# A transformer block with 16384 experts on one core: norm applied in the transposes, queries of four heads at once, residual kept on chip, six of the last sixteen V rows on VectorE

## The chip, the core and the metric

The kernel runs on one core of a Trainium2 chip. The metric is the device time of one execution in microseconds (us), median of several runs. TensorE multiplies, VectorE and ScalarE work on tiles of 128 partitions, GpSimd (POOL) here issues only DMAs whose row numbers are read from memory (gathers), SyncE (SP) issues plain DMAs. Each engine runs its own program in order; they meet at semaphores.

## The reference, cut to what matters

The block has a first half (modulation, attention, a recurrent branch, a short convolution, an output projection) that the change leaves alone but for its last stage. The second half is a layer of experts picked for each of 256 tokens:

```python
x = x + m_lat[2] * merge_branches(...)                 # the residual, "x2" below
hx = modulate(rmsnorm(x, norm_ffn), m_lat[3], m_lat[4])
x = x + m_lat[5] * peer_ffn(hx, peer_wq, peer_k1, peer_k2, peer_u, peer_v)

def peer_ffn, for 8 heads:
    q = hblk @ w_q                                     # two halves of 128 per head
    s1, s2 = q[..., 0, :] . k1, q[..., 1, :] . k2      # 128 keys each
    v1, i1 = top_k(s1, 16); v2, i2 = top_k(s2, 16)
    score, pos = top_k(v1 + v2 (16 x 16), 16)          # 16 experts of 16384
    gate = softmax(score)
    act = gelu(w_u[idx] . hblk)                        # a row of 2048 for each expert
    out += (gate * act) @ w_v[idx]                     # another row of 2048
```

For each head, token and k, one row of U and one of V (8 KB each) is read: 8 heads x 256 tokens x 16 x 2 rows, 537 MB in all.

## The kernel before, in words

The 256 tokens are two tiles of 128 (t = 0, 1). One gather brings row k of all 128 tokens of a tile: 128 x 2048 floats, 1.05 MB. There are 256 U gathers and 256 V gathers. U lands in a ring of 4 slots, V in a ring of 8. For each U gather VectorE forms the dot product with the token's normed row hN (line 1595); when the 16 of a tile are there it makes 16 weights wt (lines 1602 to 1611, with a sigmoid on ScalarE, line 1032). ScalarE makes a diagonal matrix dg from each weight (line 1039), and TensorE multiplies it with the V slot, four matmuls of 512 columns (line 736), summing in PSUM banks 0 to 3. After 16 rows VectorE adds the four banks to acc (line 1615), and the first row of the next tile waits for this add.

The last stage of the first half (WO) makes x2. TensorE uses weight pieces that ScalarE (line 781) and VectorE (line 1083) split into a high and a low part; four buffers of each lie between. Two column chunks of 512 are ready at once for both tiles: VectorE scales and adds them (lines 1504, 1506). Then, on one chain: x2 is stored to memory by ScalarE's queue (line 1005), ScalarE squares the two tiles with a sum (line 1009), a square root (line 1011), VectorE's reciprocal, hN in two halves by a multiply and an add for each tile (lines 1518, 1520), 32 transposes on TensorE (line 699) with 16 copies from PSUM on ScalarE (line 1015), the query projection of head 0 (line 711, 16 k-tiles x 2 blocks), its copy (line 1024), scores (line 722), top-k on VectorE (route, lines 1524 to 1587), and the first gather (line 1661). VectorE does the top-k of both tiles before its first dot product. The projection weights come in pieces of 1.05 MB, two per head, through four slots W by SP: head h + 2 is loaded when head h's projection has used its slots (line 377).

POOL's order is written out (lines 1655 to 1692): 16 U gathers of head 0, tile 0, with four V after the fourth; then turns, in which a U gather of one tile alternates with a V gather of the tile before. A U gather waits for the dot product that frees its slot, a V gather for the TensorE row that frees its slot; a waiting gather holds up all behind it. In the last head's second tile there are V gathers alone. At the end acc is multiplied by m5 and the residual is added, after it was read back from memory (lines 1051, 1626, 1628), and stored (line 395).

## Time and profile before

| | us |
|---|---|
| median of 3 runs | 3104.57 (3101.61 to 3104.84) |
| the profiled execution, time | 3104.09 |
| the profiled execution, span | 3102.3 |

| engine | busy us | share of the span |
|---|---|---|
| TensorE (PE) | 2675.0 | 86% |
| VectorE (DVE) | 1909.1 | 62% |
| ScalarE (ACT) | 912.5 | 29% |
| GpSimd (POOL) | 600.8 | 19% |

The span is that of the one execution whose trace is read below; its time has 1.8 us around it. Starts in the trace count from the start of the span. The first half ends at 1692.8 us, the first gather is issued at 1744.04. In a line of the timeline, the bracket at the end says how long the engine sat idle before the instruction and what released it.

### The profile page before, as it was taken

How to read it: one execution, taken by the hardware profiler on the slowest of the kernel's cores; microseconds unless marked ns; L12 is line 12 of the kernel's file. 1: busy time of each engine (PE TensorE's matmuls, PEld its weight loads, DVE VectorE, ACT ScalarE, POOL GpSimd, SP SyncE). 2: the span in 40 equal slices, each digit the busy share in tenths (PEclk: the TensorE clock that was granted, in tenths of full speed). 3: DMA queues.
4: the chain of work that ended last, by engine and by line, in shares of the span. 5: the costliest groups of instructions: out<-in, count | busy, mean ns of one | idle time of the engine just before them, and what ended most of it. 6: DMA issues, size and time to landing. Idle time of an engine off the chain costs nothing.

```text
span 3102.3 us, 32041 instructions
## 1 busy us (share of the span) xinstructions
PE 2675.0 (86%) x11089; PEld 1816.9 (59%) x11089; DVE 1909.1 (62%) x2600; ACT 912.5 (29%) x1241; POOL 600.8 (19%) x580
## 2 busy tenths in 40 slices
PE   8899997999989999999998466869697887887778
PEld 3488875878767789998876423333343343343323
DVE  2389997443665768887545566655555565566552
ACT  1167775432554333333433110101011111111100
POOL 0000000000000000000000255334353434443341
PEclk9999998999999999999999788989899899999999
DMA  8633333542424868887564699999999999999996
GB/s 331 226 126 108 122 112 132 190 165 95 143 88 160 345 265 344 344 315 285 204 240 182 249 410 407 421 412 422 421 408 421 401 422 408 422 399 421 422 421 282
DMA packets 126625, 906.83 MB, mean 292 GB/s; under 512 B 14016, under 2 KB 15552, under 8 KB 16704
## 3 DMA queue, kind: packets, MB, share of 16 engines
q0 software_dynamic: 82944, 604.02, 47.3%
q1 hardware_dynamic: 38304, 278.94, 24.2%
q10 hardware_dynamic: 5280, 22.72, 1.9%
q8 instruction: 44, 0.72, 0.1%
q14 instruction: 53, 0.43, 0.0%
HBM read 901.39 MB, written 4.23 MB: 292 GB/s over the span
## 4 chain that ended last, share of the span: by engine, by line
PE 45%; DMA 29%; DVE 12%; issue 9%; ACT 3%; POOL 1%; DVEq 0%; ACTq 0%; POOLq 0%
DMA u<-in_peer_u,idx 28%; PE ps L425 9%; PE ps L468 8%; PE ps L470 8%; PE ps L469 7%; PE ps L736 6%; PE ps L483 3%; DVE u L1595 2%; DVE wl L1083 2%; PE ps L440 1%; DVE ub L1167 1%; ACT wh L781 1%; PE ps L622 1%; POOL v L1668 1%; DVE tt L1178 1%
## 5 line engine op out<-in xcount | busy, mean ns | idle before, releaser
L736 PE MATMUL ps<-v,dg 128*128 128x512 f32 x2048 | 931.1, 611 | 195.2 <-DMA v<-in_peer_v,idx 98.6
L1595 DVE SCALAR_TENSOR_TENSOR u<-u,hN 128x2048 f32<-128x2048 f32 x256 | 586.3, 2292 | 483.8 <-DMA u<-in_peer_u,idx 472.5
L736 PEld LDWEIGHTS ps<-v,dg 128*128 128x128 f32 x2048 | 392.6, 196 | 729.4 <-issue 586.0
L1083 DVE TENSOR_TENSOR wl<-w,wh 128x1024 fp32r<-128x1024 f32 x432 | 524.8, 1222 | 414.6 <-ACT wh L781 413.8
L781 ACT ACTIVATE wh<-w 128x1024 fp32r<-128x1024 f32 x432 | 453.5, 1058 | 685.8 <-PE ps L470 418.7
L1661 POOL DMA_INDIRECT u<-in_peer_u,idx x256 | 283.7, 1108 | 878.8 <-DVE u L1595 458.0
L425 PE MATMUL ps<-both,wh 128*128 128x256 f32 x2048 | 372.2, 285 | 5.4 <-DVE y L1295 5.1
L1039 ACT ACTIVATE dg<-con,wt 128x128 f32<-128x128 f32 x256 | 99.0, 399 | 849.7 <-PE ps L736 844.6
L425 PEld LDWEIGHTS ps<-both,wh 128*128 128x128 f32 x2048 | 320.8, 193 | 10.2 <-issue 9.1
L1668 POOL DMA_INDIRECT v<-in_peer_v,idx x256 | 282.9, 1105 | 184.0 <-PE ps L736 99.9
L1653 POOL DMA_DIRECT2D mr<-in_wmod x64 | 34.0, 532 | 1401.4 <-DVE br_lo L1423 980.1
L425 PE MATMUL ps<-both,wl 128*128 128x256 f32 x1024 | 290.3, 283 | 0.0
L468 PE MATMUL ps<-wh,both 128*128 128x512 f32 x640 | 263.4, 411 | 13.8 <-DVE wl L1083 10.3
L470 PE MATMUL ps<-wh,both 128*128 128x512 f32 x640 | 251.4, 393 | 0.0
L469 PE MATMUL ps<-wl,both 128*128 128x512 f32 x640 | 251.0, 392 | 0.0
L425 PEld LDWEIGHTS ps<-both,wl 128*128 128x128 f32 x1024 | 197.2, 193 | 0.0
L440 PE MATMUL ps<-both,wh 128*128 128x512 f32 x512 | 161.8, 397 | 9.6 <-DVE both L1146 8.6
L468 PE MATMUL ps<-wh,br_hi 128*128 128x512 f32 x384 | 150.8, 393 | 4.1 <-DVE wl L1083 3.2
L469 PE MATMUL ps<-wl,br_hi 128*128 128x512 f32 x384 | 150.1, 391 | 0.0
L470 PE MATMUL ps<-wh,br_lo 128*128 128x512 f32 x384 | 150.0, 391 | 0.0
L468 PEld LDWEIGHTS ps<-wh,both 128*128 128x128 f32 x640 | 121.4, 190 | 45.9 <-DVE wl L1083 11.7
L1263 DVE SCALAR_TENSOR_TENSOR mr<-mr,srow 128x2048 f32<-128x2048 f32 x64 | 146.1, 2283 | 2.4 <-DMA mr<-in_wmod 2.4
(224 smaller groups left out, 2730.3 us busy)
## 6 DMA issues: line engine op xcount, KB each, us to landing
w<-in_stream SPq DMA_DIRECT2D x264, 1024.0 KB, 4.8
mr<-in_wmod POOLq DMA_DIRECT2D x64, 1024.0 KB, 6.8
wg<-in_gates ACTq DMA_DIRECT2D x8, 512.0 KB, 3.5
u<-in_peer_u,idx POOLq DMA_INDIRECT x256, 16.8
v<-in_peer_v,idx POOLq DMA_INDIRECT x256, 18.0
xs<-in_ctx ACTq DMA_DIRECT2D x1, 2048.0 KB, 17.1
xs<-in_x ACTq DMA_DIRECT2D x1, 2048.0 KB, 23.0
x<-in_x ACTq DMA_DIRECT2D x1, 2048.0 KB, 7.9
```

Source lines behind the costliest of these rows:

```text
L425: last = mm(ps[:, bank, c0:c0 + T], w[:, kk, cols], src[part_][:, k, :], start=(k == 0 and bank not in started), stop=(k == KT - 1), skip_ ...
L440: last = mm(ps[:, banks + blk, :].rearrange("p (s t) -> p s t", s=2), w[:, kk, cols], both[:, :, part_, k, :], start=(k == 0 and n == 0), ...
L468: mm(ps[:, bank + i, :], of[0][:, k, rows], hi[:, kk, :], start=(k == 0), stop=False)
L469: mm(ps[:, bank + i, :], of[0][:, k, rows], lo[:, kk, :], start=False, stop=False)
L470: last = mm(ps[:, bank + i, :], of[1][:, k, rows], hi[:, kk, :], start=False, stop=(k == KT - 1))
L736: last = mm(ps[:, b, :], dg[:, k % 4, :], V[n % NV][:, b * 512:(b + 1) * 512], start=(k == 0), stop=(k == TOPK - 1))
L781: fn(wh[p % SPLITS][:, :, :], W[s][:, q * PIECE:(q + 1) * PIECE, :], ACT.Copy).then_inc(hi_done, 1)
L1083: tt(wl[p % SPLITS][:, :, :], W[s][:, q * PIECE:(q + 1) * PIECE, :], wh[p % SPLITS][:, :, :].bitcast(F32), ALU.subtract)\
L1263: stt(mr[n % NM][:, :], mr[n % NM][:, :], 1.0, srow[:, :], ALU.mult, ALU.mult, accum_out=mcols[:, n:n + 1])\
L1595: stt(U[n % NU][:, :], U[n % NU][:, :], 1.0, hN[:, t, :], ALU.mult, ALU.mult, accum_out=dot[:, t, k:k + 1])\
L1661: nc.gpsimd.indirect_dma_start(out=U[n % NU][:, :], out_offset=None, in_=a_u, in_offset=bass.IndirectOffsetOnAxis(ap=idx[:, odd, t, k:k + ...
L1668: nc.gpsimd.indirect_dma_start(out=V[n % NV][:, :], out_offset=None, in_=a_v, in_offset=bass.IndirectOffsetOnAxis(ap=idx[:, odd, t, k:k + ...
```

## The change

- Norm: ScalarE squares x2 in the four column chunks, each as soon as it is final; VectorE adds the partial sums. hN is at first only x2 times the reciprocal root (tile 0 on ScalarE, tile 1 on VectorE), so that the transposes can start; the gain and the shift are applied while the transposed tiles are copied out of PSUM, with a scale and a bias per partition (gcol, mcb, from columns that VectorE made earlier), every second one on VectorE. The full hN for the dot products is made by VectorE behind the transposes. The clearing of acc and the making of the gain row gfr move up into the WO stage.
- Queries: heads 0 to 3 are projected one after another at the start, each into a PSUM bank of its own; later head h + 4 is projected in the turn of head h. The weights of heads 2 and 3 go to four new slots WX, in the place of the split buffers, as soon as the first half's last piece is used. Three query buffers instead of one.
- VectorE's first dot product comes after the top-k of tile 0; the top-k of tile 1 goes four steps ahead and then between the dot products. POOL issues 2 + 2 + 4 V gathers among head 0's first 16 U gathers, the third group behind a wait for head 3's projection, and the first turn begins with V row 8.
- Residual: x2 stays on chip, neither stored nor read back.
- Last 16 V rows (head 7, tile 1): k = 1, 3, 5, 7, 9, 11 are multiplied and added by VectorE into acc, the other ten on TensorE in banks 4 to 7, which need not wait for the add of banks 0 to 3; each bank is finished and stored by itself.
- TensorE's and ScalarE's programs for the heads are written out instead of looped.

```diff
+            sp.wait_ge(piece_used, 2 * WQ0)
+            for s in range(4):
+                sp.dma_start(WX[s][:, :, :], a_stream[WQ0 + 4 + s].rearrange("p (k n) -> p k n", n=CW)).then_inc(wx_in[s], 16)
+            for h in range(4, PH):
+                for s in (0, 1):
+                    sp.wait_ge(piece_used, 2 * (WQ0 + 2 * (h - 1 if h > 4 else 0) + s + 1))
+                    sp.dma_start(W[s][:, :, :], a_stream[WQ0 + 2 * h + s].rearrange("p (k n) -> p k n", n=CW)).then_inc(arrived[s], 16)
...
+            route(0)
             scores(0, True)
-            route(0, 2)
+            route(1)
+            route(2)
             scores(1)
-            with pe.Fori(0, PH // 2 - 1) as i:
-                for odd in (0, 1):
-                    experts(i * 2 + odd, 0)
-                    route(i + 1, 2 * odd)
-                    scores(i * 2 + (2 + odd))
-                    experts(i * 2 + odd, 1)
-            experts(PH - 2, 0, 1)
-            experts(PH - 1, 0, 1)
+            route(3)
+            pe.wait_ge(*AR.at(3, "q"))
+            for h in range(PH):
+                experts(h, 0)
+                if h + 4 < PH:
+                    route(h + 4)
+                if h + 2 < PH:
+                    scores(h + 2)
+                if h + 1 < PH:
+                    experts(h, 1)
+            last_half()
...
+            def last_half():
+
+                for j, k in enumerate(ON_PE):
+                    n = TOPK + k
+                    pe.wait_ge(v_in[n % NV], (PH - 1) * (2 * TOPK // NV * 16) + 16 * (n // NV + 1))
+                    pe.wait_ge(last_dg, j + 1)
+                    for b in range(4):
+                        last = mm(ps[:, 4 + b, :], dg[:, j % 4, :], V[n % NV][:, b * 512:(b + 1) * 512], start=(j == 0), stop=(k == TOPK - 1))
+                        if k == TOPK - 1:
+                            last.then_inc(last_bank, 1)
+                    if k < TOPK - 1:
+                        last.then_inc(last_pe, 1)
...
+            def squares(c):
+
+                for t in (0, 1):
+                    act.wait_ge(*VW.at(c // 2, f"a{c % 2}{t}"))
+                    if c:
+                        act.wait_ge(*AF.at(0, f"sq{c - 1}{t}"))
+                    fn(junk2[:, t, :], x2[:, t, c * WIDE:(c + 1) * WIDE], ACT.Square, accum_out=fsq[:, t, c:c + 1]).then_inc(*AF.inc(f"sq{c}{t}"))
...
+            squares(NW - 1)
+            act.wait_ge(*VF.at(0, "ss"))
             fn(fst[:, 2:4], fst[:, 0:2], ACT.Sqrt, scale=1.0 / D, bias=tiny[:, 1:2]).then_inc(*AF.inc("rt"))
-            act.dma_start(keys[:, :, :], a_keys[0].rearrange("p (s n) -> p s n", s=2)).then_inc(keys_in, 16)
-            for k in range(KT):
...
+            for k in range(1, KT, 2):
                 act.wait_ge(*PF.at(0, f"hT{k}"))
-                fn(hT[:, k, :], ps[:, 4 + k % 4, 0:T], ACT.Copy).then_inc(*AF.inc(f"hT{k}"))
-            act.wait_ge(*VF.at(0, "ha11"))
+                fn(hT[:, k, :], ps[:, 4 + k % 4, 0:T], ACT.Identity, scale=gcol[:, k:k + 1], bias=mcb[:, KT + k:KT + k + 1]).then_inc(*AF.inc(f"hT{k}"))
...
+            queries(0)
             gates(0, 0)
+            queries(1)
+            load_keys(1)
+            queries(2)
             gates(0, 1)
-            queries(1)
+            queries(3)
             gelus(0, 0)
-            with act.Fori(0, PH - 2) as h:
+            for h in range(PH):
                 turn(h)
-            turn(PH - 2, queries_too=False)
-            turn(PH - 1, more=False, queries_too=False)
+            act.wait_ge(*VE.at(PH - 1, "w1"))
+            for j, k in enumerate(ON_PE):
+                act.wait_ge(*(last_used(ON_PE[j - 4]) if j >= 4 else PE_.at(PH - 1, f"v0{TOPK - 4 + j}")))
+                fn(dg[:, j % 4, :], ident, ACT.Copy, scale=wt[:, 1, k:k + 1]).then_inc(last_dg, 1)
...
+                    nc.vector.memset(acc[:, :, :], 0.0).then_inc(*VF.inc("acc0"))
+                    dve.wait_ge(rows_in, 48)
+                    stt(gfr[:, :], m4r[:, :], 1.0, gfr[:, :], ALU.add, ALU.mult).then_inc(*VF.inc("g1"))
+
+            dve.wait_ge(*AF.at(0, f"sq{NW - 1}1"))
+            nc.vector.reduce_sum(fst[:, 0:2], fsq[:, :, :], AX.X).then_inc(*VF.inc("ss"))
             dve.wait_ge(*AF.at(0, "rt"))
-            nc.vector.reciprocal(fst[:, 4:6], fst[:, 2:4]).then_inc(*VF.inc("rc0"))
-            dve.wait_ge(*VF.at(0, "rc0"))
+            nc.vector.reciprocal(fst[:, 4:6], fst[:, 2:4]).then_inc(*VF.inc("rc"))
+            dve.wait_ge(*VF.at(0, "rc"))
             for half in (0, 1):
                 cols_ = slice(half * D // 2, (half + 1) * D // 2)
-                for t in (0, 1):
-                    stt(hN[:, t, cols_], x2[:, t, cols_], fst[:, 4 + t:5 + t], gfr[:, cols_], ALU.mult, ALU.mult).then_inc(*VF.inc(f"hm{t}{half}"))
-                    dve.wait_ge(*VF.at(0, f"hm{t}{half}"))
-                    tt(hN[:, t, cols_], hN[:, t, cols_], m3r[:, cols_], ALU.add).then_inc(*VF.inc(f"ha{t}{half}"))
-            nc.vector.memset(acc[:, :, :], 0.0).then_inc(*VF.inc("acc0"))
-            dve.wait_ge(*VF.at(0, "acc0"))
+                tsc(hN[:, 1, cols_], x2[:, 1, cols_], fst[:, 5:6], None, ALU.mult).then_inc(*VF.inc(f"x1{half}"))
+            for k in range(0, KT, 2):
+                dve.wait_ge(*PF.at(0, f"hT{k}"))
+                tsc(hT[:, k, :], ps[:, 4 + k % 4, 0:T], gcol[:, k:k + 1], mcb[:, KT + k:KT + k + 1], ALU.mult, ALU.add).then_inc(*VF.inc(f"hT{k}"))
+            dve.wait_ge(*PF.at(0, f"hT{KT - 1}"))
+            for t in (0, 1):
+                tt(hN[:, t, :], hN[:, t, :], gfr[:, :], ALU.mult).then_inc(*VF.inc(f"hm{t}"))
+                dve.wait_ge(*VF.at(0, f"hm{t}"))
+                tt(hN[:, t, :], hN[:, t, :], m3r[:, :], ALU.add).then_inc(*VF.inc(f"ha{t}"))
...
+            def last_row(k):
+
+                j, n = ON_DVE.index(k), TOPK + k
+                dve.wait_ge(v_in[n % NV], (PH - 1) * (2 * TOPK // NV * 16) + 16 * (n // NV + 1))
+                if j:
+                    dve.wait_ge(last_dve, j)
+                stt(acc[:, 1, :], V[n % NV][:, :], wt[:, 1, k:k + 1], acc[:, 1, :], ALU.mult, ALU.add).then_inc(last_dve, 1)
...
+            for _ in range(4):
+                next(second)
+            dots(0, 0, second)
             dots(0, 1, route(1, 0, 1, False))
...
+            last_row(1)
             add(PH - 1, 0)
-            final(0)
-            add(PH - 1, 1)
-            final(1)
+            dve.wait_ge(last_in, 16)
+            dve.wait_ge(*VA.at(PH - 1, "ac0"))
+            tt(acc[:, 0, :], acc[:, 0, :], m5r[:, :], ALU.mult).then_inc(*VX.inc("m"))
+            last_row(3)
+            dve.wait_ge(*VX.at(0, "m"))
+            tt(acc[:, 0, :], acc[:, 0, :], x2[:, 0, :], ALU.add).then_inc(*VX.inc("o"))
+            for k in ON_DVE[2:]:
+                last_row(k)
+            dve.wait_ge(last_dve, len(ON_DVE))
+            tt(acc[:, 1, :], acc[:, 1, :], m5r[:, :], ALU.mult).then_inc(*VX.inc("m1"))
+            dve.wait_ge(*VX.at(0, "m1"))
+            tt(acc[:, 1, :], acc[:, 1, :], x2[:, 1, :], ALU.add).then_inc(*VX.inc("p1"))
+            for b in range(4):
+                cols_ = slice(b * WIDE, (b + 1) * WIDE)
+                dve.wait_ge(last_bank, b + 1)
+                tt(U[0][:, cols_], ps[:, 4 + b, :], m5r[:, cols_], ALU.mult).then_inc(*VX.inc(f"x{b}"))
+                dve.wait_ge(*VX.at(0, f"x{b}"))
+                tt(acc[:, 1, cols_], acc[:, 1, cols_], U[0][:, cols_], ALU.add).then_inc(*VX.inc(f"o{b}"))
...
+                if last and n >= TOPK + NV:
+                    pool.wait_ge(*last_used(k - NV))
...
+                    rows_v(0, 0, 0, 0)
+                    rows_v(0, 0, 0, 1)
+                if k == NU + 2:
+                    pool.wait_ge(piece_used, 2 * (WQ0 + 4))
+                    rows_v(0, 0, 0, 2)
+                    rows_v(0, 0, 0, 3)
+                if k == NU + 8:
+                    pool.wait_ge(piece_used, 2 * (WQ0 + 8))
+                    for kv in range(4, 8):
                         rows_v(0, 0, 0, kv)
-            turn(0, 0, begun=4)
+            turn(0, 0, begun=8)
```

## Rows read from the trace of the kernel before

**Rows 1.** Busy time by stretch: five engines, TensorE clock share, DMA share, GB/s

```profile
1744.00:3030.00 1286.00, 970.96 (x2364) 453.63 (x2363) 762.58 (x1188) 142.73 (x321) 555.09 (x503) 0.91 1.00 414
```

**Rows 2.** Chain that ended last, gather stage: one longer link, one typical

```profile
2052.48 22.11 DMA u<-in_peer_u,idx
...
2138.68 16.75 DMA u<-in_peer_u,idx
```

**Rows 3.** Timeline of the end: POOL, VectorE, TensorE

```profile
3012.87 2.48 POOL L1668 DMA_INDIRECT v<-in_peer_v,idx  x1 [0.30 <-issue]
3027.16 2.29 DVE L1595 SCALAR_TENSOR_TENSOR u<-u,hN 128x2048 f32<-128x2048 f32 x1 [2.67 <-DMA u<-in_peer_u,idx]
3029.66 3.70 PE L736 MATMUL ps<-v,dg 128*128 128x512 f32 x8 [1.27 <-DMA v<-in_peer_v,idx]
3035.83 55.17 PE L736 MATMUL ps<-v,dg 128*128 128x512 f32 x128 [2.47 <-DVE acc L1615]
3091.04 2.29 DVE L1615 TENSOR_TENSOR acc<-acc,ps 128x2048 f32<-128x2048 f32 x1 [40.78 <-PE ps L736]
3095.68 2.29 DVE L1628 TENSOR_TENSOR acc<-acc,x2b 128x2048 f32<-128x2048 f32 x1
```

**Rows 4.** Timeline of VectorE and ScalarE after WO: x2, squares, root, hN, clearing

```profile
1694.97 0.69 DVE L1506 TENSOR_TENSOR x<-x,xm 128x512 f32<-128x512 f32 x1
1698.60 1.91 ACT L1009 ACTIVATE junk<-x 128x2048 f32<-128x2048 f32 x1
1701.91 0.29 ACT L1011 ACTIVATE fst<-fst,tiny 128x2 f32<-128x2 f32 x1
1702.44 1.28 DVE L1518 SCALAR_TENSOR_TENSOR hN<-x,fst,gfr 128x1024 f32<-128x1024 f32 x1
1713.15 3.47 DVE L1521 MEMSET acc<- 128x4096 f32 x1 [0.80 <-issue]
```

**Rows 5.** Timeline of TensorE: transposes, then head 0's queries

```profile
1707.49 3.67 PE L699 MATMUL ps<-con,hN 128*128 128x128 f32 x16 [14.73 <-DVE hN L1520]
1712.40 3.68 PE L699 MATMUL ps<-con,hN 128*128 128x128 f32 x16 [1.24 <-DVE hN L1520]
1716.55 14.08 PE L711 MATMUL ps<-hT,w 128*128 128x256 f32 x64 [0.47 <-ACT hT L1015]
```

**Rows 6.** Busy time by stretch, as in group 1: the transposes, then behind them

```profile
1707.00:1716.00 9.00, 7.27 (x32) 6.55 (x32) 8.13 (x6) 5.69 (x15) 0.00 (x0) 0.50 0.00 0
1716.00:1724.00 8.00, 7.53 (x36) 6.57 (x36) 0.62 (x1) 0.46 (x2) 0.00 (x0) 0.97 0.39 131
```

**Rows 7.** Timeline of POOL: the first gather, V row 8; landing of U by source line

```profile
1744.04 0.99 POOL L1661 DMA_INDIRECT u<-in_peer_u,idx  x1 [308.19 <-DVE tv L1531]
1817.09 2.19 POOL L1668 DMA_INDIRECT v<-in_peer_v,idx  x1 [0.30 <-PE ps L736]
...
DMA to landing us min/median/max: 5.6/8.7/15.8
```

**Rows 8.** Timeline of VectorE, end of WO: the two splits behind the second chunk

```profile
1655.87 1.23 DVE L1083 TENSOR_TENSOR wl<-w,wh 128x1024 fp32r<-128x1024 f32 x1 [0.30 <-ACT wh L781]
1658.59 1.23 DVE L1083 TENSOR_TENSOR wl<-w,wh 128x1024 fp32r<-128x1024 f32 x1 [1.49 <-ACT wh L781]
```

**Rows 9.** Page, costliest groups: ScalarE's splits

```profile
L781 ACT ACTIVATE wh<-w 128x1024 fp32r<-128x1024 f32 x432 | 453.5, 1058 | 685.8 <-PE ps L470 418.7
```

**Rows 10.** Timeline: last dot of the first tile, TensorE, ScalarE, the fifth dot after

```profile
1803.21 2.29 DVE L1595 SCALAR_TENSOR_TENSOR u<-u,hN 128x2048 f32<-128x2048 f32 x1 [0.39 <-DMA u<-in_peer_u,idx]
1807.50 50.78 PE L736 MATMUL ps<-v,dg 128*128 128x512 f32 x112 [46.97 <-ACT dg L1039]
1813.51 0.40 ACT L1039 ACTIVATE dg<-con,wt 128x128 f32<-128x128 f32 x1 [5.28 <-PE ps L736]
1826.11 2.29 DVE L1595 SCALAR_TENSOR_TENSOR u<-u,hN 128x2048 f32<-128x2048 f32 x1 [1.68 <-DMA u<-in_peer_u,idx]
```

**Rows 11.** Source line of SP's weight loads from 1700 us on: first and last

```profile
L377 SPq DMA_DIRECT2D w<-in_stream x12: 333/333/334, 1723.9 to 2395.0; - x12
```

More of the change, by code:

```diff
@@ L115, in build @@
         m_flat = m_dram.rearrange("r (c n) -> (r c) n", n=P)
-        x2_dram = nc.dram_tensor("x2_rows", [2, P, D], F32, kind="Internal").ap()
         def sem(name):
@@ L356, in build, with last_used @@
         PE_ = Steps(sem("pe_experts"), [f"v{t}{k}" for t in (0, 1) for k in range(TOPK)], primed=True)
-        VX = Steps(sem("dve_last"), ["m0", "o0", "m1", "o1"])
+        VX = Steps(sem("dve_last"), ["m", "o", "m1", "p1"] + [f"{w}{b}" for b in range(4) for w in "xo"])
+        ON_DVE = (1, 3, 5, 7, 9, 11)
+        ON_PE = tuple(k for k in range(TOPK) if k not in ON_DVE)
+        last_pe, last_dve, last_bank, last_dg = sem("last_pe"), sem("last_dve"), sem("last_bank"), sem("last_dg")
+        def last_used(k):
+            return (last_dve, ON_DVE.index(k) + 1) if k in ON_DVE else (last_pe, ON_PE.index(k) + 1)
         PRIMED_V = [VM, VT, VL] + VO + [VS, VW, VE, VA]
@@ L700, in _, with route @@
                 last.then_inc(*PF.inc(f"hT{k}"))
-            pe.wait_ge(*AF.at(0, f"hT{KT - 1}"))
-            def route(turn, slot0):
+            def route(h):
                 for q in (0, 1):
-                    s = slot0 + q
-                    pe.wait_ge(arrived[s], turn * 16 + 16 * (WQ0 // RING + 1))
+                    if h < 2:
+                        w, in_, n = W[2 * h + q], arrived[2 * h + q], 16 * (WQ0 // RING + 1)
+                    elif h < 4:
+                        w, in_, n = WX[2 * h + q - 4], wx_in[2 * h + q - 4], 16
+                    else:
+                        w, in_, n = W[q], arrived[q], 16 * (WQ0 // RING + h - 2)
+                    pe.wait_ge(in_, n)
+                    if h > 4 and q == 0:
+                        pe.wait_ge(*AR.at(h - 1, "q"))
                     for kk in range(HK):
                         k = q * HK + kk
+                        if h == 0:
+                            pe.wait_ge(*evicted(k))
                         for blk in (0, 1):
-                            last = mm(ps[:, 4, blk * T:(blk + 1) * T], W[s][:, kk, blk * P:(blk + 1) * P], hT[:, k, :],
+                            last = mm(ps[:, min(h, 4), blk * T:(blk + 1) * T], w[:, kk, blk * P:(blk + 1) * P], hT[:, k, :],
                                       start=(k == 0 and blk == 0), stop=(k == KT - 1), skip_group_check=True)
@@ L1000, in _ @@
                 split(WO0, 0, 16, p)
+                if p == 14:
+                    squares(0)
             for p in range(5, 16):
                 split(WO0, 1, 16, p)
[L1003 to L1009 removed]
@@ new lines, in _, with load_keys @@
+            act.wait_ge(*VF.at(0, "rc"))
+            for half in (0, 1):
+                cols_ = slice(half * D // 2, (half + 1) * D // 2)
+                fn(hN[:, 0, cols_], x2[:, 0, cols_], ACT.Copy, scale=fst[:, 4:5]).then_inc(*AF.inc(f"x0{half}"))
+            def load_keys(h):
+                if h:
+                    act.wait_ge(*PR.at(h - 1, "s1"))
+                act.dma_start(keys[:, :, :], a_keys[h].rearrange("p (s n) -> p s n", s=2)).then_inc(keys_in, 16)
+            load_keys(0)
@@ L1678, in turn @@
                         rows_u(h + 1, 1 - odd, 0, k)
-                    rows_v(h, odd, 1, k)
-            pool.wait_ge(*VF.at(0, "ha11"))
+                    rows_v(h, odd, 1, k, not more)
             for k in range(TOPK):
```

114 lines of the change are left out of this document (53 added, 61 removed).

## The prediction

> **What bounds the kernel now.** I read the busy time by stretch first. From the first gather to the last dot product (1744 to 3030) the DMA engines are busy all the time, 414 GB/s on average, and TensorE has air [rows 1]. The chain of waits says the same: U gathers of mostly 16.75 us between short steps [rows 2]. A gather is 1.05 MB; dot products at the end of the stage start every 4.97 us (2.29 busy, 2.67 idle) and cover one U and one V gather [rows 3], so one transfer takes 2.5 us. Three parts have to be costed: what lies ahead of the first gather, what the DMA engines carry or miss until the last dot, and the tail behind it, where 128 matmuls run without a pause [rows 3] and only TensorE counts.
>
> **A, the way to the first gather: 10 us less.** Before: x2 is complete at 1695.66; squares, table load and root run to 1702.20; four multiply and add pairs lie between 1702.44 and the second half of the transposes at 1712.40; head 0's queries start at 1716.55 [rows 4, 5]. After: the last chunk's square of 512 columns costs a quarter of 1.91 us and some 0.3 around it, to 1696.5. The root comes 1.4 us behind the last square as before (1700.51 to 1701.91, a table load in it; the small sum of VectorE hides behind that load), and ends at 1698.2. Reciprocal 0.25; scaling the first half on two engines at once at most 1.28 (the old multiply did more). Transposes start at 1699.7 and not 1707.49: 7.8 us less. They lose the pause of 1.24 us and the last copy's 0.47 [rows 5]: 1.7 less. Copies go to two engines, so TensorE stays the slower. The clock is granted at 0.50, so 1.2 GHz, during both halves and 0.97 behind them [rows 6]; it rose when the second 16 transposes had run without a pause. Here all 32 do, so I take 2.4 GHz by the queries at the latest, with some of the transposes quicker (up to 2 us). Sum 7.8 + 1.7 + 0.5 = 10. From the queries' end (1730.63) to the first gather lie 13.4 us of scores and top-k [rows 5, 7]; this is as before. Bounds: nothing lost from the clock and 2 us won, -12; the queries entirely at 1.2 GHz cost 14 us more, +4.
>
> The full hN, four operations of 2.3 us on VectorE, begins behind the transposes at about 1707 and ends at 1716; VectorE is next wanted when the queries and scores are through, at 1722. Cost nothing, cover 6 us.
>
> The clearing of acc (3.47 us [rows 4]) and gfr (2.3 like every VectorE operation of 2048 columns) go into WO, ahead of the split of piece 21 [rows 8]. Without them that split starts at 1655.87, with them 5.8 later at 1661.6, and it ends at 1662.8. TensorE needs the piece five pieces of 2.72 us after the chunk's end at about 1649.2 (the second split's 1658.59 is the same distance behind the first, 2.72), so at 1662.8. It just fits; later splits win back 1.49 us each [rows 8]. I take 0; if the cover is short, up to 2 us. ScalarE's squares, 1.6 us a chunk, fit beside splits of 1.06 in 2.72 [rows 9]. The removed stores of x2 were on no one's path but POOL's V gathers, which came later.
>
> **B, the start of the gathers: 8.5 us more.** G is the first gather's start. A first landing takes 5.6 us [rows 7]. TensorE's queries of heads 1 to 3 and two scores (3 x 14.1 + 2 x 1.2 = 44.7 us from 13.4 before G) end at G + 31.3. POOL waits for them behind U12, which waits for dot 8; U8 is the 13th transfer, lands at G + 35.6 and its dot ends at G + 38. So this wait costs nothing. But POOL's first turn now starts with U'0 (tile 1), then V8, and V8 waits for the first TensorE row of head 0. Transfers ahead: 16 U, 8 V, U'0. With 2.5 us each U15 lands at G + 63, its dot ends at T = G + 65.5, and U'0 has landed by then too. From the last dot's end (1805.43) TensorE starts 2.1 us later, and its first row frees the slot 6.0 us after that, at 1813.51 [rows 10]. V8 is then issued at T + 8.3 = G + 73.8 and lands at G + 79.4. U'1 is queued behind V8 on POOL, so VectorE has nothing either. The DMA engines stand idle from G + 65.6 to 76.9, 11 us.
>
> Before, V8 was issued at G + 73.1 in a full queue and the dot on U'4 began at G + 82.1 [rows 7, 10]; V8, one transfer ahead, landed at G + 79.6. So at the same distance from G, the kernel before has 20 U and 9 V, the new one 17 U and 9 V. It lacks three gathers, 7.5 us; with 1 us for the slower filling between top-k steps 8.5. Bounds: 0 (if the queue is somehow never dry) and 11 + 1.
>
> **C, weights: 5.4 us less.** SP issues twelve pieces from 1723.9 to 2395.0 [rows 11]: heads 2 to 7. Those of heads 4 to 7 come during the gathers; each pair makes one link of the chain 22.11 instead of 16.75 us, so 5.4 a pair [rows 2]. In the new kernel heads 2 and 3 are loaded from 1692.8 and head 4 behind head 0's queries, with idle DMA engines; heads 5 to 7 remain. One pair less. (The piece of head 3 that fell just behind the first gather is in the count of B, which compares with what really landed.)
>
> **D, the tail: 20.3 us less.** L is the last dot's end, 3029.4 before (3027.16 + 2.29). The kernel before ends at L + 72.9. Now V0 of the last tile (issued 3012.87) is next in the queue behind V15 of tile 0, used at L + 0.3 [rows 3], so V0 lands at L + 2.7 and Vk 2.5k later, V15 at L + 40.2, if its slot is free. Slots: TensorE ends tile 0 at L + 4.0, then row 0 at 7.5 (3.45 us a row, 55.17 / 16), 2 at 11.2, 4 at 16.2, 6 at 21.2; VectorE does row 1 to 7.5, the add and the first multiply to 12.1, row 3 to 14.4, the second add, rows 5 to 19.0 and 7 to 22.5. V15's slot is free at 22.5, 17.7 us before V15 would land; the queue stays full. The removed read-back of x2 (2.1 MB) no longer stands in that queue. TensorE then follows the landings: rows 8, 10 end at 26.2, 31.2, row 12 at 36.1, and 13, 14, 15 back to back at 39.6, 43.0, 46.4. VectorE is through with row 11 and two whole-row operations at 37.1. Bank 0 is ready at 44.0; four banks of two operations of 0.69 us and a little around them, 5.8, give L + 50. The last store is 4.3 us for 1.05 MB before (3097.97 to the span's end); a quarter of the bytes saves 1.9: L + 52.6. So 72.9 - 52.6 = 20.3. Bounds: 17 to 23.
>
> A gather's issue took 0.99 us with VectorE in short steps, 2.19 beside dot products [rows 7]; the tail now has VectorE at work there. Eight late issues cost at most 10 us, under the 17.7 in hand. The Trainium skill, page SBUF — State Buffer, section "SBUF: two separate sides", says that a VectorE operation with two SBUF inputs and a GpSimd operation that reads SBUF exclude each other for their whole length. By that rule VectorE's own rows would wait as well and the tail could lose some us; the issue row agrees in kind.
>
> **The sum.** -10 + 8.5 - 5.4 - 20.3 = -27.2 from the profiled execution's 3104.09 (span 3102.3 and 1.8): 3076.9, said as 3077. The execution is 0.5 under the median of the runs, so the two can be compared.
>
> **Rivals.** (1) The queue doesn't run dry at the start: PE's first row or POOL's order turns out harmless. Against: the wait stands in program order. 3077 - 8.5 = 3068.5. (2) The clock stays low into the queries. For: 0.50 right up to 1716 [rows 6]. Half of the queries at 1.2 GHz is 7 us: 3084. (3) The tail pays: VectorE and POOL exclude each other, ten operations each 0.9 us later, then the banks begin late: 3084; should the six rows save nothing beyond TensorE's freed wait (the change doesn't do what it says), 13 us of TensorE rows come back: 3090. (4) Slower: POOL's dry queue returns at each of the fifteen later tile turns, because V gathers wait for TensorE and U gathers lie behind them. It needs 27.2 / 15 = 1.8 us of idle DMA at each to undo everything; at 3 us each the time is 3122. Against: the turns' order is unchanged from head 1 on, and the share was 1.00 there [rows 1]. TensorE's longer program, written out, could do the same by fetching; no row shows it.
>
> **Chances.** Forecast 0.68, (1) 0.10, (2) 0.08, (3) 0.08 with 0.03 of it at 3090, (4) 0.04; a mix of (2) and (3) near 3100 has 0.02. Range 3065 to 3087: it holds the forecast with its bounds (about 7 us either way), (1), (2) and the milder part of (3). 0.2% of the time, 6 us, is about what a measurement of this kernel can tell from no change: faster 0.94, within 0.02, slower 0.04.
>
> **What would show it.** Right: transposes starting about 1700 and the first gather at 1734; DMA share near 0 for some 11 us around G + 70 and a wait of POOL for TensorE there; three links of 22 us instead of four; the last dot near 3022.6; TensorE's last row 46 us behind it. Wrong: a first gather later than 1738 (A), no dry stretch (B), a DMA share under 0.98 in later turns (rival 4), TensorE rows in the tail waiting for dg or a landing longer than 1.6 us each (D), or TensorE waiting for a split near 1662 in WO.

## The result, and the profile after

| | before | after |
|---|---|---|
| median of the runs, us | 3103.2 (4 runs, 3101.61 to 3104.84) | 3082.11 (4 runs, 3080.03 to 3083.83) |
| ratio, 95% interval | | 0.993 [0.9915, 0.9946] |
| the profiled execution, time and span, us | 3104.09, 3102.3 | 3083.66, 3081.8 |
| busy: TensorE, VectorE, us | 2675.0, 1909.1 | 2660.0, 1930.2 |
| busy: ScalarE, GpSimd, us | 912.5, 600.8 | 912.0, 599.6 |

The change saves 21 us, where 27 had been forecast; 3082.1 lies inside the range of 3065 to 3087. Four points cut both spans into the parts of the prediction: the end of x2, the first gather G, the end of the last dot product L, and the end of the span.

| us | before | after | difference | forecast |
|---|---|---|---|---|
| end of x2 | 1695.66 | 1692.73 | -2.9 | 0 |
| end of x2 to G | 48.38 | 36.31 | -12.1 | -10 (A) |
| G to L | 1285.41 | 1298.07 | +12.7 | +8.5 - 5.4 = +3.1 (B, C) |
| L to the end | 72.85 | 54.69 | -18.2 | -20.3 (D) |

So the total is off by 6 us and would be off by more: a miss of 10 us in the middle is half covered by the first two rows, and the 2.9 us of the first are chance, as the repeated traces below show. Each row has to be looked at for itself.

**The way to the first gather.** The timeline of the kernel after, ScalarE and TensorE, where [rows 4, 5] answer for before; then the busy time by stretch as in [rows 6] (stretch, its length, busy time of PE, PEld, DVE, ACT, POOL, granted clock, DMA share, GB/s):

```profile
1692.76 0.63 ACT L1051 ACTIVATE junk<-x 128x512 f32<-128x512 f32 x1 [0.73 <-DVE x L1575]
1694.80 0.29 ACT L1063 ACTIVATE fst<-fst,tiny 128x2 f32<-128x2 f32 x1
...
1696.53 5.55 PE L720 MATMUL ps<-con,hN 128*128 128x128 f32 x32 [6.71 <-ACT hN L1067]
1701.91 13.98 PE L740 MATMUL ps<-hT,w 128*128 128x256 f32 x64
```

```profile
1696.50:1699.00 2.50, 2.47 (x12) 2.47 (x13) 1.37 (x4) 2.04 (x3) 0.00 (x0) 0.50 1.00 423
1699.00:1702.00 3.00, 3.00 (x23) 2.44 (x22) 2.63 (x6) 2.71 (x6) 0.00 (x0) 0.93 0.95 391
```

The transposes start 3.80 us behind the end of x2 (11.83 before), and 32 of them with the change to the queries take 5.38 us (9.06 before). The clock stood at 0.50, that is 1.2 GHz, for the first of them and at 0.93 on average from 1699 on, mostly 2.4 GHz, after TensorE had worked without a pause from 1696.53. When it rises differs between executions of the same instructions: in nine traces of kernels with these transposes (all but the one with the squares behind x2, below) they took 5.3 to 5.4 us in seven and 6.2 to 6.3 us in two.

**The start of the gathers.** The timeline of the kernel after: POOL's first two gathers of the first turn, U'0 (the prime marks tile 1) and V8, then dot 15 and the dots of U'0 and U'1 on VectorE, and TensorE's first rows:

```profile
1786.22 0.94 POOL L1755 DMA_INDIRECT u<-in_peer_u,idx  x1 [0.31 <-issue]
1807.80 0.94 POOL L1765 DMA_INDIRECT v<-in_peer_v,idx  x1 [20.65 <-PE ps L765]
...
1797.14 2.29 DVE L1670 SCALAR_TENSOR_TENSOR u<-u,hN 128x2048 f32<-128x2048 f32 x1 [0.19 <-DMA u<-in_peer_u,idx]
1800.66 2.28 DVE L1670 SCALAR_TENSOR_TENSOR u<-u,hN 128x2048 f32<-128x2048 f32 x1
1816.67 2.29 DVE L1670 SCALAR_TENSOR_TENSOR u<-u,hN 128x2048 f32<-128x2048 f32 x1 [13.72 <-DMA u<-in_peer_u,idx]
...
1801.43 43.33 PE L765 MATMUL ps<-v,dg 128*128 128x512 f32 x96 [41.35 <-ACT dg L1100]
```

This is the cycle that was forecast: V8 waits 20.65 us for TensorE's first row, U'1 stands behind V8, and VectorE waits 13.72 us for U'1. What it costs is read from the busy time by stretch, cut at equal distances from the first gather: G to G + 68, to 82.1, to 120, to 172, then the rest of the stage. First after:

```profile
1729.04:1797.04 68.00, 31.03 (x148) 27.09 (x146) 42.87 (x68) 3.48 (x6) 34.42 (x25) 0.76 0.96 383
1797.04:1811.14 14.10, 9.71 (x19) 4.33 (x20) 5.39 (x9) 2.30 (x7) 1.88 (x2) 0.71 0.18 60
1811.14:1849.04 37.90, 33.62 (x79) 14.61 (x77) 19.01 (x35) 3.69 (x7) 19.52 (x16) 1.00 1.01 414
1849.04:1901.04 52.00, 29.74 (x96) 18.95 (x96) 37.14 (x56) 4.82 (x13) 27.80 (x19) 0.80 0.94 375
...
1900.00:3026.00 1126.00, 871.66 (x2024) 389.94 (x2024) 656.98 (x1021) 128.83 (x288) 468.13 (x440) 0.92 1.00 414
```

and the same four stretches of the kernel before:

```profile
1744.04:1812.04 68.00, 8.84 (x25) 5.37 (x24) 49.58 (x78) 3.77 (x9) 43.32 (x27) 0.55 0.96 383
1812.04:1826.14 14.10, 14.10 (x34) 6.25 (x33) 8.32 (x20) 1.60 (x4) 11.66 (x9) 1.00 1.01 426
1826.14:1864.04 37.90, 35.83 (x83) 15.22 (x81) 24.55 (x41) 5.96 (x12) 13.07 (x13) 1.00 1.01 422
1864.04:1916.04 52.00, 22.69 (x86) 16.95 (x87) 31.69 (x47) 1.97 (x6) 23.64 (x18) 0.74 1.00 411
```

Up to G + 68 both move 383 GB/s. Then the new kernel moves 60 against 426 GB/s for 14.1 us: 5.16 MB less, at the stage's 414 GB/s 12.5 us. The third stretch adds 0.3 MB, 0.7 us; the fourth, where the share is 0.94 and not 1.00, 36 x 52 = 1.9 MB, 4.5 us. Together 7.3 MB, 17.7 us. From 1900 on the share is 1.00, as in [rows 1].

Not all of these bytes are gathers. SyncE's timeline of the kernel before has a weight piece of 1.05 MB (head 3's second) behind its first gather at 1744.04; in the kernel after, all pieces up to head 4's are issued before the first gather:

```profile
1746.47 0.33 SPq L377 DMA_DIRECT2D w<-in_stream  x1
```

So of the 17.7 us, 2.5 are this piece, which the new kernel need not load here, and 15.2 are missing gathers: 4 of them up to G + 82.1 (29.6 against 25.6).

**The weights.** The chain of waits, its links over 19 us in the gather stage of the kernel after (columns start, length, what), then the first such link of the kernel before:

```profile
1888.94 20.07 DMA u<-in_peer_u,idx
...
2053.73 22.12 DMA u<-in_peer_u,idx
...
2221.99 22.09 DMA u<-in_peer_u,idx
```

```profile
1889.21 18.46 DMA u<-in_peer_u,idx
```

Each starts between 0.3 us before and 14 us after SyncE issues a pair of pieces (1875.36, 2053.83 and 2222.11 after; 1875.31, 2052.79, 2219.51 and 2388.07 before). Before there were this link of 18.46 and three like the first of [rows 2], for four pairs; after there are three: one pair less.

**The tail.** The timeline of the kernel after, TensorE, VectorE, POOL's issue of V8 and SyncE, where [rows 3] answer for before; L is 3027.11:

```profile
3030.86 3.60 PE L776 MATMUL ps<-v,dg 128*128 128x512 f32 x8
3051.86 24.19 PE L776 MATMUL ps<-v,dg 128*128 128x512 f32 x48 [3.43 <-DMA v<-in_peer_v,idx]
...
3047.20 2.35 DVE L1703 SCALAR_TENSOR_TENSOR acc<-v,wt,acc 128x2048 f32<-128x2048 f32 x1 [1.16 <-DMA v<-in_peer_v,idx]
3054.56 2.35 DVE L1703 SCALAR_TENSOR_TENSOR acc<-v,wt,acc 128x2048 f32<-128x2048 f32 x1 [5.01 <-DMA v<-in_peer_v,idx]
3073.51 0.69 DVE L1736 TENSOR_TENSOR u<-ps,m5r 128x512 f32<-128x512 f32 x1 [6.97 <-PE ps L776]
3078.22 0.69 DVE L1738 TENSOR_TENSOR acc<-acc,u 128x512 f32<-128x512 f32 x1
...
3035.27 0.95 POOL L1765 DMA_INDIRECT v<-in_peer_v,idx  x1 [2.50 <-DVE acc L1703]
...
3043.81 0.34 SPq L412 DMA_DIRECT2D out<-acc  x1
```

```profile
3051.00:3055.00 4.00, 3.14 (x4) 1.51 (x5) 0.44 (x1) 0.00 (x0) 0.60 (x1) 0.51 1.01 426
```

V8 of the last tile is used at L + 24.75 and not 22.7. TensorE idles 3.43 us before it, VectorE then 5.01, and in the next 4 us the granted clock is 0.51. SyncE had issued the store of out[0], 1.05 MB, at 3043.81: 8.5 us behind the issue of V8, but 8 us ahead of V8's use. (POOL's line names VectorE's row 1 as what released V8; its slot is that of row 0 on TensorE, which ended 0.3 us before.) TensorE's last row ends at L + 48.9, VectorE's last add at L + 51.8.

### The profile page after: what moved, and what is told of

The parts are those of the page before. It is cut to its first block, busy times and chain, and to the rows that moved or that the text cites. A ratio compares the mean times of both kernels' runs of the same rounds, so it can differ in the third digit from the quotient of the medians.

```text
span 3081.8 us, 31629 instructions
## 1 busy us (share of the span) xinstructions
PE 2660.0 (86%) x11041; PEld 1807.1 (59%) x11041; DVE 1930.2 (63%) x2622; ACT 912.0 (30%) x1241; POOL 599.6 (19%) x580
## 4 chain that ended last, share of the span: by engine, by line
PE 44%; DMA 29%; DVE 12%; issue 9%; ACT 3%; POOL 1%; DVEq 0%; ACTq 0%; POOLq 0%
DMA u<-in_peer_u,idx 27%; PE ps L445 9%; PE ps L488 7%; PE ps L490 7%; PE ps L489 7%; PE ps L765 5%; PE ps L503 3%; DVE u L1670 2%; DMA v<-in_peer_v,idx 2%; DVE wl L1148 2%; POOL v L1765 1%; PE ps L460 1%; ACT wh L827 1%; DVE ub L1232 1%; PE ps L642 1%
## 5 line engine op out<-in xcount | busy, mean ns | idle before, releaser
L765 PE MATMUL ps<-v,dg 128*128 128x512 f32 x1920 | 882.2, 616 | 188.5 <-DMA v<-in_peer_v,idx 92.7
L765 PEld LDWEIGHTS ps<-v,dg 128*128 128x128 f32 x1920 | 370.7, 197 | 695.9 <-issue 538.0
L1755 POOL DMA_INDIRECT u<-in_peer_u,idx x256 | 270.1, 1055 | 856.0 <-DVE u L1670 447.5
L1765 POOL DMA_INDIRECT v<-in_peer_v,idx x256 | 295.3, 1154 | 198.0 <-PE ps L765 111.5
```

Of the source, the lines that this page charges most:

```text
L765: last = mm(ps[:, b, :], dg[:, k % 4, :], V[n % NV][:, b * 512:(b + 1) * 512], start=(k == 0), stop=(k == TOPK - 1))
L1755: nc.gpsimd.indirect_dma_start(out=U[n % NU][:, :], out_offset=None, in_=a_u, in_offset=bass.IndirectOffsetOnAxis(ap=idx[:, odd, t, k:k + ...
L1765: nc.gpsimd.indirect_dma_start(out=V[n % NV][:, :], out_offset=None, in_=a_v, in_offset=bass.IndirectOffsetOnAxis(ap=idx[:, odd, t, k:k + ...
```

## The experiments

The theory after these traces: the time is gained on three paths, each counting one to one (A, C, D), and half of it is given back because V8, second in the first turn, starves the DMA engines. The rivals: the first turn is slow for another reason (POOL's issues beside VectorE, the DMA engines themselves); the shorter way to G is hidden; the rows on VectorE do nothing. Medians stand beside those of the kernel before in the same series: 3105.74 us (7 runs) for the first four kernels, 3103.41 (7 runs) for the next three, 3102.82 (7 runs) for the last two. The kernel after has two series of its own, 3082.11 beside 3103.2 and 3079.43 beside 3102.82, so a difference of 2 to 3 us between medians of different series says nothing; G to L and the tail, read from the traces, are steadier. The edits are against the kernel after.

**No block of V gathers ahead of the turn.** V8 is no longer the first V gather of the turn, V4 is, and its slot has never been used:

```
-                if k == NU + 8:
-                    pool.wait_ge(piece_used, 2 * (WQ0 + 8))
-                    for kv in range(4, 8):
-                        rows_v(0, 0, 0, kv)
-            turn(0, 0, begun=8)
+            pool.wait_ge(piece_used, 2 * (WQ0 + 8))
+            turn(0, 0, begun=4)
```

> The changed kernel with one thing put back: POOL issues only V rows 0 to 3 among head 0's first 16 U gathers, and the first turn begins with U'0, V4, U'1, V5 and so on, so that V8 is the fifth V gather of that turn and four U gathers of tile 1 go ahead of it. Theory (the dry queue): the loss at the start comes from V8 standing in front of U'1 while it waits for TensorE's first row. Then the DMA share has no dry stretch at the end of head 0's first tile, POOL's wait of 20.65 us there shrinks to under 5 us, and the time is that of the changed kernel less 11 to 18 us: 3064 to 3071. Rival (the filling): the loss comes from the top-k of tile 1 between the first dot products, which slows the U ring whatever POOL's order is; then the dry stretch only moves and the time is within 4 us of 3082.

Measured: 3064.96 us (3062.66 to 3067.43), ratio 0.9868 [0.9851, 0.9884]; 17 us less than the kernel after, 20 if each is compared with the kernel before in its own series. Busy time by stretch, G = 1733.03:

```profile
1801.03:1815.13 14.10, 14.10 (x34) 6.27 (x33) 8.17 (x13) 1.60 (x4) 11.66 (x9) 1.00 1.01 425
1815.13:1853.03 37.90, 34.63 (x80) 14.76 (x79) 22.64 (x42) 5.56 (x11) 12.18 (x13) 1.00 1.01 422
1853.03:1905.03 52.00, 22.78 (x86) 16.72 (x85) 31.96 (x46) 2.21 (x7) 22.78 (x17) 0.70 1.00 411
```

The dry stretch is gone, and so is the dip at G + 120 to 172. These are the numbers of the kernel before to within 1 GB/s. G to L is 1277.83, 20.2 less than after. Over all traces it is 1292.9 to 1298.1 (mean 1294.9) in the five kernels with this block and POOL's order unchanged, and 1276.5 to 1277.8 (mean 1277.4) in the three without it: the block costs 17.5 us. Against the kernel before it is 7.6 less, which is three weight pieces at 2.5 us: C's pair, and head 3's piece that fell behind G. So without the block nothing is lost at the start.

**U gathers first, the block kept.** Four U' gathers go ahead of V8, in the order in which their slots come free; all eight early V gathers stay:

```
-                for k in range(TOPK):
-                    rows_u(h, odd, 1, k)
-                    if k + begun < TOPK:
-                        rows_v(h, odd, 0, k + begun)
+                if begun:
+                    for k in range(NU):
+                        rows_u(h, odd, 1, k)
+                    for k in range(NU, TOPK):
+                        if k - NU + begun < TOPK:
+                            rows_v(h, odd, 0, k - NU + begun)
+                        rows_u(h, odd, 1, k)
...
```

> The changed kernel, but in the first turn the four U gathers of tile 1 whose slots are free go ahead of V8; the eight early V gathers stay. Theory (the dry queue): three more transfers lie in the queue while TensorE makes its first row, so 3 x 2.5 = 7.5 us of the 11 us dry stretch are filled and some 3 us of it stay: 3073 to 3076. If the pause of 12.0 us before dot 13, behind the block of four V gathers, is a cost of its own, four_early is another 3 to 8 us faster than this one; if it is not, the two differ by the 3 us only. Rival (the filling): within 4 us of 3082.

Measured: 3070.88 us (3069.62 to 3072.06), ratio 0.9888 [0.9871, 0.9904], 2 us under the expected range. POOL's timeline at the turn, then the stretch from G + 68 to 82.1 (G = 1731.48):

```profile
1796.41 2.49 POOL L1755 DMA_INDIRECT u<-in_peer_u,idx  x1 [7.37 <-DVE u L1670]
1809.59 2.45 POOL L1765 DMA_INDIRECT v<-in_peer_v,idx  x1 [6.96 <-PE ps L765]
```

```profile
1799.48:1813.58 14.10, 10.98 (x20) 4.85 (x21) 11.76 (x22) 2.30 (x7) 6.54 (x4) 0.71 0.70 241
```

POOL stands 6.96 us for TensorE instead of 20.65. The stretch still lacks (425 - 241) x 14.1 = 2.6 MB, 6.3 us, and the time is 5.9 us above the kernel without the block. So the order is two thirds of the loss. The rest stays as long as eight V gathers come early, which is the cost of its own that the expectation put at 3 to 8 us: the tile's last dot ends at G + 69.1 here and at G + 58.9 with four early V gathers, and TensorE's first row starts at G + 71.1 and not at 60.9.

**The store of out[0] later.** It waits for tile 1's second whole-row operation on VectorE, the last one before the banks, and so is no longer in flight beside the last V gathers:

```
-            sp.wait_ge(*VX.at(0, "o"))
+            sp.wait_ge(*VX.at(0, "p1"))
             sp.dma_start(out[0], acc[:, 0, :]).then_inc(stored, 16)
```

> The changed kernel, but the store of tile 0's output (1.05 MB) waits until tile 1's rows on VectorE are in and its first two whole-row operations are done, so that it no longer lies among the last V gathers. Theory: that store takes 2.5 us of the DMA engines just ahead of V row 8 of the last tile, which lands 2 us late; TensorE stands still for 3.4 us, its clock falls to 0.51 and row 8 runs at half speed. Without the store V8 lands 2.5 us earlier, the clock stays at 1.00, and from the last dot product to the end of the span it takes 52 us and not 54.7: a gain of 2 to 4 us, 3078 to 3080 in time. Rival: the landing is late because POOL's issues wait for VectorE (1.9 us each instead of 0.9); then V8's landing, the pause and the 54.7 us stay as they are.

Measured: 3077.67 us (3077.62 to 3078.62), ratio 0.9912 [0.9896, 0.9929]. TensorE's timeline and the busy time of the end; L is 3023.61:

```profile
3056.08 14.00 PE L776 MATMUL ps<-v,dg 128*128 128x512 f32 x32 [1.26 <-DMA v<-in_peer_v,idx]
```

```profile
3049.00:3055.00 6.00, 4.57 (x11) 1.48 (x9) 3.41 (x2) 0.55 (x2) 0.00 (x0) 1.00 1.03 425
```

Row 8 now starts at L + 22.6 (24.75 with the early store), though POOL issues V8 at the same L + 8.2 in both, and its issues beside VectorE still take 1.9 us: so it was the store, not POOL. The last row ends at L + 46.5, the forecast's 46.4; the clock stays at 1.00, and the tail is 52.19 us, 2.5 less. It is 52.2 in the three traces with the later store and 54.6 to 54.7 in the six with the early one and six rows on VectorE. The median fell by 4.4, the rest of it ahead of L, where nothing was edited.

**All sixteen last rows on TensorE.** The banks, the early store and the residual on chip stay:

```
-        ON_DVE = (1, 3, 5, 7, 9, 11)
+        ON_DVE = ()
...
-            last_row(1)
...
-            last_row(3)
```

> The changed kernel with all sixteen last V rows on TensorE, in banks 4 to 7 and without VectorE's six rows; the output by banks and the on-chip residual stay. Theory: TensorE's 16 rows of 3.45 us then run from 4 us behind the last dot without a pause, to L + 59, and the span ends at L + 65 to 66: 11 us more than the changed kernel, 3092 to 3094, and 7 us less than the kernel before, which is the share of the banks, of the store and of the residual. Rival: the V landings are the bound in the tail (the last one at about L + 42), so that sixteen rows on TensorE cost 3 to 5 us only: 3085 to 3087.

Measured: 3089.84 us (3087.91 to 3092.3), ratio 0.9953 [0.9936, 0.997]; tail 64.56 us. TensorE's timeline, L = 3021.54:

```profile
3025.28 55.10 PE L776 MATMUL ps<-v,dg 128*128 128x512 f32 x128
```

The median is 2 us under the expected 3092 to 3094 and the tail 0.4 under the expected 65: against the two series of the kernel after it is 7.7 and 10.4 us longer. The sixteen rows run without a pause and set the end. The six rows on VectorE are worth 64.56 - 54.69 = 9.9 us, and 12.4 with the later store. What is left of D, 72.85 - 64.56 = 8.3 us, can be read from the traces: the rows start at L + 3.7 and not at 6.4, without the wait for the add of banks 0 to 3 (2.6 us), and from their end to the span's end it takes 5.7 us and not 11.3 (5.6 us). How much of the 5.6 belongs to the finishing by banks, to the split store and to the residual kept on chip was not taken apart.

**Both fixes at once.** The first and the third edit:

> The changed kernel with both edits at once: only four V gathers ahead of the first turn, and the store of out[0] behind the issue of the last V gathers. The dry queue cost 17.2 us and the store 2.5 (tail 54.7 against 52.2 in the kernel with the later store alone); they lie in different stages, so the two should add: 3065.0 - 2.5 = 3062.5 us, a DMA share of 0.90 to 1.0 through the first tile turn and a tail of 52.2 us with TensorE at a granted clock of 1.0. A rival: the earlier last dot finds the store's place taken by something else, and the sum of the two is smaller: 3065.

Measured: 3063.14 us (3062.94 to 3065.51), ratio to the kernel before 0.9871 [0.9855, 0.9888]; the tail is 52.23 us. It beats the kernel before by 40 us and the changed one by 19. That it beats the kernel without the block by the whole 2.5 us isn't shown by the times (1.8 apart, with overlapping runs), only by the tails, 52.23 against 54.64.

**All squares at the end of ScalarE's program.**

```
-                if p == 14:
-                    squares(0)
...
-                if p in (6, 14):
-                    squares(p // 8 + 1)
-            squares(NW - 1)
+            for c in range(NW):
+                squares(c)
```

> The changed kernel, but ScalarE takes all its squares of x2 behind the last chunk instead of three of four between the splits. Theory, that the way to the first gather counts one to one: eight squares of about 0.63 us with some 0.2 around each stand between x2 and the root instead of two, so the transposes start 4.9 us later behind the end of x2 (8.7 instead of 3.8), the first gather 4.9 later behind it, the rest of the span as before, 3087. A rival: the first gathers are waited for by something else, or the splits gain what ScalarE no longer does beside them, and the time stays at 3082.

Measured: 3081.03 us (3080.78 to 3081.84), ratio 0.993 [0.9913, 0.9946]: no loss. The expected 3087 was wrong. ScalarE's timeline:

```profile
1683.47 0.62 ACT L1051 ACTIVATE junk<-x 128x512 f32<-128x512 f32 x1
1691.71 0.63 ACT L1051 ACTIVATE junk<-x 128x512 f32<-128x512 f32 x1 [7.53 <-DVE x L1572]
```

Six squares ran up to 1684, in the 11 us in which ScalarE, with all its splits done, waits for the last chunk. Where three of the four chunks are squared doesn't matter; that the last chunk alone is left does. The test added nothing to the path and says nothing of it.

**All squares behind the end of x2.** The same with a wait ahead, in the kernel with both fixes:

```
+            act.wait_ge(*VW.at(1, "a11"))
             for c in range(NW):
                 squares(c)
```

> Both fixes as in the kernel both_fixes, and all eight squares of x2 held back until x2 is complete. In squares_last the first six still ran before that, in ScalarE's idle 11 us ahead of the last chunk, and the time stayed. Here eight squares of 0.615 us each start at the end of x2, 4.99 us with 0.07 ahead of them; the last square ended 0.76 behind the end of x2 so far, so everything behind it begins 4.2 us later. Theory, one to one on the path: first gather 40.5 us behind the end of x2 instead of 36.3, and the time 3063.1 + 4.2 = 3067.3. A rival, that some of the way to the first gather is hidden: between 3063 and 3065.

Measured: 3067.01 us (3066.39 to 3072.1), ratio 0.9883 [0.9867, 0.99]; 3.9 us over the kernel with both fixes. The busy time during the transposes and behind them:

```profile
1707.00:1710.00 3.00, 2.78 (x13) 2.79 (x14) 1.87 (x4) 2.33 (x4) 0.00 (x0) 0.50 0.38 150
1710.00:1713.20 3.20, 3.20 (x22) 2.91 (x21) 2.44 (x6) 2.51 (x5) 0.00 (x0) 0.76 0.00 0
```

The first gather is issued 41.1 us behind the end of x2 and not 36.3: 4.3 from the squares, 0.5 because the clock rose later within the transposes, which it also does by 0.9 us between executions of unchanged code and so can't be put down to the edit. From G to L the two kernels differ by 1.2 us (1277.76 and 1276.54). So, within the 1 us by which such traces differ, the way to the first gather lies on the path one to one, and a saved microsecond there is a microsecond of the time.

**Without the query weights of heads 5 to 7.** Their queries use the weights of head 4, so six pieces of 1.05 MB aren't loaded and these heads pick other experts, by as many gathers of the same size:

```
-            for h in range(4, PH):
+            for h in range(4, 5):
...
-                        w, in_, n = W[q], arrived[q], 16 * (WQ0 // RING + h - 2)
+                        w, in_, n = W[q], arrived[q], 16 * (WQ0 // RING + 2)
```

> The changed kernel without the loads of the query weights of heads 5, 6 and 7; their queries are made with the weights of head 4, which are in the slots. So those heads pick other experts, but as many gathers of the same size run. Left out are six transfers of 1.05 MB. Theory: while the DMA engines are busy throughout, each pair costs 5.4 us, its link in the chain of waits being 22.1 instead of 16.7: three links of 22 us become 16.7, and the time is 3082 - 16.2 = 3066. A rival: the loads slip into idle DMA time and TensorE or VectorE set the pace, then it stays within 5 us of 3082.

Measured: 3064.73 us (3064.62 to 3067.84), ratio 0.9877 [0.986, 0.9893]: 17.4 us less than the first series of the kernel after and 14.7 less than the second, 16.2 expected. The chain of waits where the two long links of 22 us were:

```profile
2049.14 17.12 DMA u<-in_peer_u,idx
...
2211.62 17.18 DMA u<-in_peer_u,idx
```

The third link, 20.07 at 1888.94, is 15.05. The three links are shorter by 5.0 us each, and G to L is 1280.06, 14.8 under the mean of the five traces with the same order of the gathers. So a pair, two transfers of 2.5 us in a DMA queue that is never empty, costs 5.0 us, a little under the 5.4 that I took.

**The changed kernel once more.**

> The changed kernel once more, unaltered. The end of x2 lay 2.9 us earlier in its first trace than in the trace of the kernel before, and the stretch from the first gather to the last dot product was 1298.1 us, but 1295.3 and 1295.0 in two kernels that do the same up to there. Theory: neither is the change's work. The time stays at 3082 within 2 us, the end of x2 lies anywhere from 1692 to 1699, and the stretch is 1293 to 1298 us. A rival: both numbers come again within 0.3 us, and then they belong to the code.

Measured: 3079.43 us (3076.75 to 3081.79), ratio 0.9926 [0.991, 0.9943]. Both the time and the end of x2 missed their expectation: 2.7 us under 3082 and not within 2, and 1689.87, outside 1692 to 1699. Over the ten profiled executions of changed kernels the end of x2 lay between 1689.87 and 1699.14, though they share the code up to there but for the place of the squares; and G to L was 1293.17. Neither the 2.9 us at the end of x2 nor the last 5 us of G to L belong to the change. Where the first half's spread comes from stays open; no experiment was made on it.

## Why the prediction was right or wrong, point by point

**What bounds the kernel: right.** From 1900 to the last dot the DMA share is 1.00 at 414 GB/s in both kernels, and six transfers less save about 15 us, six times 2.5.

**A: right, 2 us short.** -12.1 against -10, a tenth beyond the better of the bounds, -12 (in two other traces, with the clock rising later, -11.2). The start of the transposes came 8.0 us nearer to x2 (forecast 7.8). Transposes to queries gave 3.7 and not 2.2: the clock rose within the transposes, which was the bound and not the value I took. From the queries to G it was 27.1 us after 27.5. Rival (2), the clock low into the queries, didn't happen. The edits in WO: the split of a later piece starts late once, by 0.65 us (ScalarE's wait for TensorE is 2.31 where 1.66 is the rule, at 1662.72), inside the 0 to 2 that I gave. The trace's other 2.9 us, the earlier end of x2, are spread.

**B: the mechanism right, the size wrong by a factor of two.** The sum asks for G to L without C: 12.7 + 5.4 = 18.1 us (14.8 over the five traces with the same order), forecast 8.5, upper bound 12. V8 did wait for TensorE, U'1 behind it, so rival (1) is out, and the DMA engines idled 0.82 x 14.1 = 11.6 us where I had said 11. The step that failed is the next one, "It lacks three gathers, 7.5 us", in two ways that work against each other. First, the count of the kernel before has an order wrong: POOL issues U'4 at 1815.84 and V8 behind it at 1817.09, so V8 landed behind G + 82.1 and not at 79.6, and the count there is 20 U and 8 V. Second, the forecast let the new kernel go into the pause with too long a lead: 25 gathers by G + 65.6, where the kernel before, by its bytes, has 23. U15, the 24th transfer, landed at G + 68 and not at 63, for the mean rate up to there was 383 GB/s and not 414; T came at G + 70.4 and not 65.5, and the lead was one gather. A pause worth 4.9 gathers less a lead of one is 4 gathers, 10 us, up to G + 82.1, where three and 7.5 us stood in my sum. What the sum lacked altogether is the dip at G + 120 to 172, 4.5 us. With 0.7 us between the two it makes 15.2 us, near the 14.8 of the five traces; the other 3 of the 18.1 us lie further back, where the traces of one and the same order differ by up to 5. The pause itself, 11 us plus a restart, stood in my text as a bound and would have been the better price. Rival (4), the pause at every later turn, didn't happen: the share is 1.00 from 1900 on, also with TensorE's longer program.

**C: right, 0.4 us too much.** One pair less. The experiment without three pairs gives 14.7 to 17.4 us by the medians and 14.9 by the three links, for 16.2: 5.0 us a pair and not 5.4. Not every pair has a link of 22 us, as I wrote: head 4's had 18.46.

**D: right, 2 us too much.** -18.2 against -20.3, within 17 to 23. TensorE ended tile 0 at L + 3.9 (forecast 4.0), V8 came at 24.75 (22.7), the last row ended at 48.9 (46.4). The step that failed: "The queue stays full" was true, but I had only V gathers in it. The store of out[0], 1.05 MB, uses the same DMA engines, and V8, issued 8.5 us before it, still landed 2.2 us late; it was costed nowhere. The kernel before has this store beside its last V gathers too (issued at 3050.29), but there TensorE's rows ran back to back and waited for no landing. The pause then took the clock down, 0.51 and 0.63 in the next two stretches of 4 us, but that cost only some 0.3 us more: the last row ends 2.5 us later than with the late store. With the store later it came at 46.5. Rival (3) didn't happen: VectorE's rows took 2.35 us each beside POOL's issues of up to 1.96 us, and the rows saved 9.9 us. The Trainium skill, page SBUF — State Buffer, section "SBUF: two separate sides", has whichever of the two starts first hold the port for its whole instruction. In the trace POOL's issues in the tail double from 0.94 to 1.9 us beside VectorE, which agrees. That VectorE would wait as well doesn't show: its operations follow each other from 3034.64 to 3046.04 while POOL issues five gathers, and its 2.35 is near the 2.29 of a dot product. The loss falls on the engine with slack.

**The sum.** By the spans -20.5 against -27.2: A and the spread at the end of x2 gave 5.0 more, B took 9.6 more (of which some 3 are spread), D gave 2.1 less. That the total is not further off is in part luck: the 2.9 us at the end of x2 are no one's work. By the medians of both series of the kernel after, -21.1 and -23.4.

## What to carry to other kernels

An engine that issues gathers in program order must not meet a slot's wait before it has issued those gathers whose slots are free: filling a ring to its last slot early turns the next gather into a wait for the consumer, and puts everything behind it. Price a pause of the bounding engine by its idle time unless the lead with which it is entered is known, and check it by bytes moved at equal distances, taking out those that only one of the kernels has to move. Where work is moved or added, cost its transfers in the queue of the engine that bounds, stores too: here a store of 1 MB beside the last loads cost as much as a load.

## What the runs showed of the hardware

- 50 us behind the pause of 11.6 us of the DMA engines, 36 GB/s were missing over 52 us (375 against 411). The order of the issues gives a reason: with eight V gathers early, the first turn's last eight U gathers have no V gather between them, and each waits for a dot to free one of four slots; with four early, only the last four do. With eight early but four U gathers ahead, where again four are alone, it was 404. Whether it follows from the order alone or from the pause too wasn't tested by itself.
- A plain store takes its share of the DMA engines from gathers that were issued before it: V8, issued 8.5 us before the store of out[0], landed 2.2 us late, and V7, issued 3.4 us before V8, in time (its use at L + 20.1 with either store).
- The granted clock can fall on a short pause: TensorE idled 3.43 us in the tail, and 0.51 followed; with idles of 1.26 us between rows, and in the kernel before with one of 2.47 us, it stayed at 1.00.
- The first half ended between 1689.9 and 1699.1 us over ten profiled executions of kernels that share its code up to the squares. A difference of 3 us there between two traces doesn't show an effect of a change.
